# Expert weights w1 and w3 with eight neighbouring rows on a partition, and a token gather that takes every eighth column

## The reference, cut to what matters

```python
def hier_moe(u, lp):                      # x: 384 tokens x 1024
    x = u.reshape(-1, dm)
    ...                                   # each token picks one of 4 groups, and 2 of its 4 experts
    gate = (jax.nn.one_hot(sel, N_GROUPS, dtype=F32)[:, :, None] * inner[:, None, :]).reshape(-1, N_EXPERTS)
    hid = jax.nn.silu(jnp.einsum('nd,edf->nef', x, lp['moe_w1'])) * jnp.einsum('nd,edf->nef', x, lp['moe_w3'])
    y = jnp.einsum('nef,efd->nd', hid * gate[:, :, None].astype(hid.dtype), lp['moe_w2'])
    return y.reshape(bsz, seqlen, dm)
```

## Time and profile before

| | us |
|---|---|
| median of 3 runs | 1477.38 |
| lowest and highest | 1476.19, 1479.19 |
| profiled execution, its own time | 1473.72 |
| its span in the trace | 1471.9 |

### The profile page before, as it was taken

The page is one execution under the profiler, slowest core; times in us unless marked ns, Lnnn a source line. Parts: engine busy times, 40 slices in busy tenths (PEclk is TensorE's granted clock), DMA queues, the critical chain, the costliest instruction groups (busy, mean ns, idle before and its releaser), DMA issues. The chain is left out here.

```text
span 1471.9 us, 27399 instructions
## 1 busy us (share of the span) xinstructions
PE 1269.1 (86%) x12154; PEld 822.2 (56%) x12154; DVE 506.2 (34%) x1329; ACT 279.8 (19%) x683; POOL 37.3 (3%) x65
## 2 busy tenths in 40 slices
PE   3799997887788979999978999878988979999974
PEld 3455555677685555455434555558885555455432
DVE  0103148344535270101114032947555260101113
ACT  2012152222321121011001124232321121011002
POOL 2000000000000020000000000000000000000000
PEclk9899975899998989999998998579889989999997
DMA  9755450244260516676616232000000506676611
GB/s 349 201 200 202 152 192 0 91 142 167 73 175 2 171 30 228 228 241 217 228 61 177 87 103 56 1 1 4 4 9 2 171 0 228 229 239 218 228 58 44
DMA packets 135678, 191.74 MB, mean 130 GB/s; under 512 B 16563, under 2 KB 100768, under 8 KB 135168
## 3 DMA queue, kind: packets, MB, share of 16 engines
q1 hardware_dynamic: 132256, 179.32, 37.0%
q0 software_dynamic: 2032, 6.23, 1.4%
q10 hardware_dynamic: 1264, 4.33, 0.7%
HBM read 187.63 MB, written 2.23 MB: 129 GB/s over the span
## 5 line engine op out<-in xcount | busy, mean ns | idle before, releaser
L1125 PE MATMUL bank<-ring,region 128*128 128x512 f32 x512 | 224.8, 592 | 0.0
L1205 ACT ACTIVATE region<-bank 128x256 f32<-128x256 f32 (+5 forms) x318 | 130.3, 430 | 432.1 <-PE bank L1146 105.8
L1125 PEld LDWEIGHTS bank<-ring,region 128*128 128x128 f32 x512 | 95.9, 190 | 112.6 <-issue 111.0
L1954 DVE SCALAR_TENSOR_TENSOR region<-region,bank 128x256 f32<-128x256 f32 x32 | 15.4, 481 | 333.9 <-ACT region L1462 333.9
L1146 PE MATMUL bank<-ring,region 128*128 128x512 f32 x256 | 111.2, 592 | 0.0
L1764 DVE COPY_PREDICATED region<-lev,bank 128x512 f32<-128x512 uint8 (+1 forms) x90 | 61.0, 678 | 121.4 <-PE bank L772 120.9
L967 PE MATMUL bank<-u,ring 128*128 128x384 f32 x288 | 95.9, 491 | 0.0
L1556 DVE SCALAR_TENSOR_TENSOR h<-bank,mod,h 128x128 f32<-128x128 f32 (+1 forms) x160 | 56.4, 411 | 103.7 <-PE bank L1041 62.3
L1041 PE MATMUL bank<-u,ring 128*128 128x384 f32 x256 | 86.3, 500 | 5.9 <-DVE u L1847 5.9
L1146 PEld LDWEIGHTS bank<-ring,region 128*128 128x128 f32 x256 | 48.0, 190 | 57.4 <-issue 57.4
L876 PE MATMUL bank<-ring,cond 128*32 128x128 f32 x1536 | 54.8, 296 | 24.8 <-issue 12.5
(11 more groups left out here) (272 smaller groups left out, 1627.3 us busy)
## 6 DMA issues: line engine op xcount, KB each, us to landing
ring<-in_moe_w SPq DMA_DIRECT2D x96, 1024.0 KB, 6.9
ring<-in_w_mod SPq DMA_DIRECT2D x48, 1024.0 KB, 8.6
ring<-in_w_in SPq DMA_DIRECT2D x20, 768.0 KB, 9.0
ring<-in_w_in SPq DMA_DIRECT2D x12, 256.0 KB, 6.4
region<-in_bands POOLq DMA_DIRECT2D x2, 1280.0 KB, 7.6
ring<-in_w_out SPq DMA_DIRECT2D x4, 576.0 KB, 4.4
ring<-in_w_out SPq DMA_DIRECT2D x8, 288.0 KB, 6.2
ring<-in_w_out SPq DMA_DIRECT2D x6, 384.0 KB, 6.6
```

The source lines that it names most:

```text
L1125: last = pe.matmul(bank[j % 2][:, :], xs[:, job % 2, c, :], w[:, c, :], start=(c == 0), stop=(c == KT - 1))
L1205: return act.activation(dst, src, ACT.Copy)
```

## The change

w1 and w3 are laid out otherwise. Row 8 p + c now lies on partition p: eight neighbouring rows of a matrix, 8 KB that are contiguous in HBM, go to one partition, w1 to the first half of the slot and w3 to the second. To match it, block c of the gathered tokens must hold features c, c + 8, c + 16 and so on, so the stationary operand of the gather reads every eighth column of `u_tok`, a step of 32 bytes. The moving operand of `hidden` now reads two runs of 256 columns that lie 8 KB apart, and writes the same 512 columns of the bank. The sum over features is the same sum in another order. Items, slots, waits and the order of instructions on all engines are unchanged, and so are w2, `down` and `scatter`.

```diff
                     if m < EPG:
-                        dst = w.rearrange("p (c n) -> p c n", c=KT)
                         for half, name in enumerate(("moe_w1", "moe_w3")):
-                            sp.dma_start(dst[:, :, half * DE:(half + 1) * DE],
-                                         expert(name, l, e0 + m).rearrange("(c p) n -> p c n", p=P)).then_inc(landed, 16)
+                            sp.dma_start(w[:, KT * DE * half:KT * DE * (half + 1)],
+                                         expert(name, l, e0 + m).rearrange("(p c) n -> p (c n)", p=P)).then_inc(landed, 16)
...
                     for c in range(KT):
                         for t in range(NT):
-                            last = pe.matmul(bank[2 + c // 4][:, tc(c % 4)], u_tok[:, t, tc(c)], sel[:, b, t, :],
+                            last = pe.matmul(bank[2 + c // 4][:, tc(c % 4)], u_tok[:, t, c:D:KT], sel[:, b, t, :],
                                              start=(t == 0), stop=(t == NT - 1))
...
-                    w = item_in("job", l, JOB_ITEMS * job + j).rearrange("p (c n) -> p c n", c=KT)
+                    w = item_in("job", l, JOB_ITEMS * job + j).rearrange("p (m c n) -> p c m n", m=2, c=KT)
...
                     for c in range(KT):
-                        last = pe.matmul(bank[j % 2][:, :], xs[:, job % 2, c, :], w[:, c, :],
+                        last = pe.matmul(bank[j % 2][:, :].rearrange("p (m n) -> p m n", m=2), xs[:, job % 2, c, :], w[:, c, :, :],
                                          start=(c == 0), stop=(c == KT - 1))
```

## The result

| | before | changed |
|---|---|---|
| median, us | 1478.29 (4 runs) | 1516.50 (4 runs) |
| lowest and highest, us | 1476.19, 1481.78 | 1514.73, 1519.62 |
| profiled execution, us | 1473.72 | 1516.88 |
| its span, us | 1471.9 | 1515.1 |

The changed kernel is slower: 1.0258 times before, with a 95% interval of 1.0232 to 1.0285.

The account below looks back on a forecast made before the run. TensorE's single queue was taken to bound the expert part. Transfers and moving operand at 0 plus 353 gather records x 106.7 ns = 37.7 us, on 1477.4, gave 1515 us, range 1474 to 1527.

Parts of the forecast that it names:

- The bound: Expert part: one TensorE queue, so extra gather or `hidden` time adds to the end; shorter transfers landing in time save nothing.
- The transfers: w1/w3 DMAs: 8 KB runs land in about 6.5 us, about 1 us sooner, hidden, so costed at nothing.
- rival 3: Fourth expert's w1/w3 pair lands after its 14.0 us slot; at double 10.3 us it costs 53 us, 1530; chance 0.05.
- rival 2: First gathers: full clock from their start would give back 3.5 us, 1474; chance 0.07.
- The moving operand: `hidden`: 512 columns in two runs cost 0, at most 1 ns in 512 records, 0.5 us.
- The gather: Gather's stationary load, stepped by 32 bytes: +106.7 ns on 353 records, 37.7 us; chance 0.55.
- rival 1: Gather: the stepped load is free and transfers stay hidden, 1477 (1474 to 1481); chance 0.33.
- the signs: Full-clock gather records 200 to 240 ns apart, gather 10 to 11 us, loads above 190 ns, `hidden` 429 ns, no DMA wait.
- half rate: Gather's stepped load takes 2 x 107 = 213 ns, pitch 218 ns, +106.7 ns a record.
- DVE's row: L1885's 16-byte step: read 1.8 times as long (30.5 us in gathers) or 1.90 ns per new place (48 us).
- The lower clock level: First gather of each layer: 17 and 14 records at 1.2 GHz, nothing added; 41 us if half rate held there.
- The total: Whole kernel: 1477.4 + 37.7 = 1515 us, this case's own range 1504 to 1527.

Follow-up runs that it names:

- the run with the permuted read: Changed kernel, but ACT sorts the features once when copying token tiles from PSUM (32-byte step), so gathers load neighbours: 1475.66 us, 1.001 times before.
- the first set: First runs of the kernel before and the changed kernel, four each: medians 1478.29 and 1516.50 us, 1.0258 times before.
- The second set: The changed kernel unaltered, run again as the yardstick beside its variants: 1522.62 us median, 1.0328 (1.0297 to 1.0360) times before.

## Why the prediction was right, and what it mis-sized

- **The bound** held: TensorE is the one queue of the expert part, and 45.4 us more in the gathers are 45.1 us more in the experts.
- **The transfers** were costed at nothing with a landing of about 6.5 us; it is 6.6, and the run with the permuted read shows the whole layout at 1.001. Late transfers (rival 3) and time given back (rival 2) are out.
- **The moving operand** was costed at nothing; with one run instead of two the experts change by 0.13 us of 253, which is within their repeat.
- **The gather** was the right place, and rival 1, the free load, is out: undoing the step alone removed the loss. Contention with the transfers is no rival for the cause: the first gather of layer 1 runs at 240 ns a record with the DMA engines at a share of 0.00, a later one at 238 ns with 0.49 (rows below). Of the signs, the pitch of 200 to 240 ns came true at its upper end, and the gather of 10 to 11 us was passed, at 11.4. The term was too small. I took half rate, 106.7 ns a record more; it is 126.4 (238.1 - 111.7), 36.4 us instead of 30.7 in the six gathers at full clock. DVE's row had it: 1.90 ns for each new place there, 1.86 (238.1/128) here. Of the two ways to carry that row over, as a ratio of speeds or as a time, the time came nearer. That the two numbers are so close may be chance: they belong to different engines, L1885 also writes 12 results where its companions write 3, and no run tried DVE.
- **The lower clock level.** I added nothing for records at that level, on the ground that a plain load takes as long there; that was nearly so. In the first gather of layer 1 the granted clock over the first half was 0.50, over the second 0.94, and about as many records passed in each, as in a gather at full clock in layer 0 (us, PE busy, PEld busy, clock, DMA, GB/s; a record that reaches over the edge counts on both sides):

```profile
583.20:594.60 11.40, 11.36 (x48) 11.40 (x48) 1.00 0.49 185
1223.10:1228.90 5.80, 5.75 (x24) 5.79 (x25) 0.50 0.00 0
1228.90:1234.70 5.80, 5.80 (x26) 5.77 (x25) 0.94 0.00 0
```

  The 48 records take 11.54 us, 240 ns each, against 238 at full clock: the stepped load hardly follows the clock, while the plain one takes 213 ns at the lower level (the trace of before, 541 to 544 us; I had reckoned with 223) and 111.7 at the full. So the stepped records lose some 27 ns at the lower level too. The two first gathers lost 4.31 and 4.64 us, 8.9 together, where 65 records at 106.7 ns gave 6.9.
- **The total.** 37.7 us were forecast, the gathers cost 45.4, and the first set's medians differ by 38.2. That the forecast of 1515 stands so near 1516.5 is in part luck: the sum was 7.7 us too small, but the median of before rose to 1478.3 with its fourth run, and the stretches outside the experts drift by several us from one execution to the next. The second set (1.0328, 48.9 us between the medians) errs to the other side of 45.
- **The rule of the Trainium skill** that I set beside the rows ("Advanced Engine Details and Errata", section "SBUF Cachelines") has a line of 16 bytes and wants two hits on it. For float32 operands of TensorE the steps agree with both: step 2, with two hits a line, costs 119 ns against 112, step 4 with one hit 233.

## What to carry to other kernels

Before an operand of TensorE is read with a step, count the 16-byte lines that it touches and compare some 1.8 ns a line (1.7 to 2.1 by the steps measured here) with what stands beside it: a stepped load is free under a pass of 512 columns and doubles the time of one with 128. If a layout needs such a step in a loop, sort the data once where an engine with spare time copies it anyway. And a better transfer is worth nothing where no wait on it stands in the profile, so its price elsewhere should be looked for first.

## What the runs showed of the hardware

- A stationary operand in float32 costs about 1.8 ns for each new 16-byte line (119, 175 and 233 ns for 128 values with steps 2, 3 and 4). The moving operand costs the same (228 ns for 128 values with step 4, 451 and 900 ns for 512 with steps 2 and 4), and when both step the two don't add (240 ns).
- That time hardly follows TensorE's clock: 240 ns a record in a gather whose first half ran at a granted 0.50, 238 ns at 1.00.
- Beyond step 4 the load of 128 values lies between 218 ns (step 16) and 268 (step 12), in no order of the step. The rule behind this stays open.
- A stepped load of 128 values is hidden under a pass of 512 plain columns (432 ns a record, against 429), and sets the pace beside 256 (239 ns).
- ACT read PSUM with a step of 32 bytes as fast as without one (six copies of 512 columns in 3.04 us either way), but wrote SBUF with a step of 512 bytes at some 0.9 us a copy (5.47 us for six).
